# One core, a hybrid pooling and attention block: the value projection goes tile by tile, and ScalarE alone forms the modulated rows from the third tile on

## The chip, the core and the metric

The kernel runs on one core of a Trainium2 chip. That core has TensorE (PE in the profile, with its weight loads as PEld), VectorE (DVE), ScalarE (ACT), GpSimd (POOL) and the queue that issues most of its transfers, SyncE (SP). Every engine takes its own instructions strictly in the order in which they are written, and engines wait for one another with semaphores. The metric is the device time of one execution in microseconds (us).

## The reference, cut to what matters

One layer of a diffusion trunk, with 1024 latent tokens (8 tiles of 128 rows) and 256 context tokens (2 tiles), width 1024:

```python
hx = _rmsnorm(x, norm1[l]) * (1.0 + cx1) + sx1
hc = _rmsnorm(ctx, norm1[l]) * (1.0 + cc1) + sc1
yx, yc = _mixer(hx, hc, w_in[l], w_gk2[l], b_gk[l], w_pool[l], pool_scale[l], gla_gain[l], w_out[l], keep_ctx)
x = x + gx1 * yx
hx = _rmsnorm(x, norm2[l]) * (1.0 + cx2) + sx2
x = x + gx2 * _moe(hx.reshape(-1, D), w_router, router_bias, w1[l], w3[l], w2[l]).reshape(x.shape)
```

`_mixer` multiplies hx and hc by w_in and splits the product into u (pooling branch), q, k, v, the gate g and a rank-32 part r. From r come the decays (a small product, a log sigmoid, a cumulative sum over each chunk). A chunked linear attention with a state runs over q, k, v; its gated output and the pooled u go through w_out. `_moe` is a mixture of 16 experts, two for each token. The six modulation vectors (cx1, sx1, gx1 and so on) are silu(c) times w_mod plus a bias. All of it is float32.

## The kernel before, in words

**Precision by splitting.** A large product is made of three passes of a rounded format: a matrix is split into a high part (ScalarE copies it into the rounded format) and a low part (VectorE subtracts the high part from the original), and high*high, high*low and low*high are summed in one PSUM bank. So every group of the projection is 8 chunks of the inner dimension times 3, 24 matmuls, lines 1428 (v and g: one token tile against 256 columns) and 1431 (u, k, q: 128 columns against 512 or 256 tokens).

**Before the projection** (0 to 40 us) the first four 512-column pieces of w_mod (the shift and scale of the first norm) arrive by transfer and are multiplied with silu(c).

**The rows.** For each token tile t: `square(t)` on ScalarE sums the squares, GpSimd forms the reciprocal root, `scale_rows(t)` on VectorE scales the tile, and `turn_rows(t)` on TensorE (8 transposes, line 1355) writes it to PSUM banks 2 and 3. `hx_out(t)` then applies the modulation chunk by chunk: VectorE reads bank 2 (four instructions, line 905), ScalarE bank 3 (four instructions, line 646). `hx_high(t)` on ScalarE and `hx_low(t)` on VectorE split the result. The two banks are used once per tile, so turn_rows(t+1) waits until hx_out(t) is done.

**The projection loop.** All engines run over the same list of steps n, one projection group each (54 in all, the last 8 within the state phase). The list before is v (10 tiles for the first 256 columns, n = 0 to 9, then 10 tiles for the others, n = 10 to 19), u (n = 20 to 27), k (28 to 33), q (34 to 37), g (38 to 45, and 46 to 53). In the list each engine does, at step n, its share of several pipelines that are shifted against each other:

- TensorE: `late_turn`, then `proj(n)`, then turn_rows(n+2), `rank_rows` (r for several tiles, line 1401), `logits(n-10)` (line 1446) and `cumulate(n-13)` (line 1456).
- ScalarE: hx_out(n+2), `evacuate(n-1)` (line 700), hx_high(n+2), square(n+4), `decay_exp` (lines 680 to 684), `decays` (lines 669 to 673), `part_high` (line 659: the high half of the next columns of w_in).
- VectorE: hx_out(n+2), evacuate(n-1), scale_rows(n+3), hx_low(n+2), `softplus` (line 978), `late_row`, `late_sum`, steps of the pooling filter (`pool_steps`, lines 988 to 1022), and last `part_low` (line 915).

v groups are evacuated from PSUM by ScalarE (even tiles) and VectorE (odd tiles), u and g by ScalarE, k and q by VectorE. Banks 0 and 1 alternate for v, and from n = 20 on four banks are used, which is why the first u groups wait for `softplus` to have left banks 2 and 3.

**The late modulation.** The other eight 512-column pieces of w_mod arrive in 32 quarters of 512 KB (`load_late`, two buffers). `late_sum(q)` on VectorE multiplies and adds each quarter (two instructions, lines 951 and 953), `late_turn(i)` on TensorE (line 1465) sums over the partitions after each fourth quarter, and `late_row(i)` (line 966) adds the bias. The list `QUARTERS` says at which step n VectorE takes each quarter. TensorE's late_turn(i) waits for the last quarter of its piece (the semaphore increment at line 958) and for late_row(i-1).

**w_in in parts.** The columns of w_in come in eight parts of 1 MB (m = 0, 1: v; 2, 3: u; 4: k; 5: q; 6, 7: g), each split in two pieces (m, i). There is one high buffer and two low ones. `piece_free` says when the high buffer's piece may be overwritten, `pieces_at` at which step this is done.

**After the loop** comes the state phase (line 1486 transposes k, line 1498 multiplies it with v, VectorE carries the state; one g group runs in each of its steps), then attention outputs and the output projection, the routing, and from about 500 us on the experts (line 1644).

Of the kernel before, what the change touches and what calls it, by code (L numbers as in the profile page):

```python
# [23 lines left out]
F32 = mybir.dt.float32  # L24
# [6 lines left out]
P = 128  # L31
# [43 lines left out]
def hybrid_block(nc, x, c, ctx_in, c_ctx, w_mod, b_mod, norm1, norm2, w_in, w_gk2, b_gk, w_pool,  # L75
                 pool_scale, gla_gain, w_out, w_router, router_bias, w1, w3, w2, norm_f, inv_counts, out):
    with ExitStack() as stack:
# [47 lines left out]
        ROWS = NT - 1  # L125
        rows_at = [O_Q + t * D for t in range(ROWS)] + [O_V + NX * HALF]
        assert O_Q + ROWS * D == O_V
# [4 lines left out]
        with nc.sbuf_tensor("lead_u", [P, O_U], F32), nc.sbuf_tensor("rank_w", [P, KC, RANK2], F32) as w_r:  # L132
            pass
        sq0 = at(O_U + 256, None, D)
# [133 lines left out]
        NV = 2 * NT  # L268
        PB = 4

        def bank_of(n):

            return n % 2 if n < NV else n % PB

        def bank_before(n):

            if n < NV + 2:
                return n - 2
            return {NV + 2: -1, NV + 3: -1}.get(n, n - PB)

# [26 lines left out]

        def piece_free(m, i):

            if by_rows(m) and by_rows(m - 1):  # L310
                return (S["half_used"], m // 4 + 1) if i == 0 else (S["proj_done"], part_end[m - 1])
            if by_rows(m) or by_rows(m - 1):
                return S["proj_done"], part_end[m - 1]
            return S["proj_done"], block_end(m - 1, i)

        pieces_at = {}
        for m in range(1, len(parts)):
            for i in range(2):
                last = part_end[m - 1] if by_rows(m) or by_rows(m - 1) else block_end(m - 1, i)
                pieces_at.setdefault(last - 1, []).append((m, i))  # L320
# [13 lines left out]
        group_no = {g: n for n, g in enumerate(groups)}  # L334
# [60 lines left out]
        def _(sp):  # L395
# [7 lines left out]
            def load_part(m):  # L403
                if m >= 2:
                    sp.wait_ge(S["proj_done"], part_end[m - 2])
                col = parts[m][1]
                sp.dma_start(raw_part[m % 2].rearrange("p (k n) -> p k n", k=KC), win_v[:, :, col:col + HC]).then_inc(part_loaded[m % 2], 16)
# [15 lines left out]
            for t in range(2, NT):  # L423
                load_rows(t)
            load_part(1)
            for q in range(len(QUARTERS)):
                for m in range(2, 6):
                    if q == {2: 2, 3: 12, 4: 19, 5: 27}[m]:
                        load_part(m)
                load_late(q)  # L430
            load_part(6)
# [183 lines left out]
        def _(act):  # L615
# [24 lines left out]
            def hx_out(t):  # L640
                if t == 0:
                    act.wait_ge(S["mod_ready"], 2)
                which = 0 if t < NX else 1
                act.wait_ge(S["turned"], t + 1)
                for k in range(4, KC):
                    ins = act.activation(hx_full[t][:, k, :], ps[:, 3, (k - 4) * P:(k - 3) * P],
                                         ACT.Identity, bias=mod[:, 0, k, which:which + 1], scale=a1[:, k, which:which + 1])
                ins.then_inc(S["hx_a"], 1)

            def hx_high(t):  # L650
                act.wait_ge(S["hx_a"], t + 1)
                act.wait_ge(S["hx_v"], t + 1)
                act.activation(hx_h[:, t], hx_full[t], ACT.Copy).then_inc(S["hx_high"], 1)

            def part_high(m, i):
                act.wait_ge(part_loaded[m % 2], 16 * (m // 2 + 1))
                if m >= 1:
                    act.wait_ge(*piece_free(m, i))
                act.activation(piece(high_part[:, :], m, i), piece(raw_part[m % 2], m, i), ACT.Copy).then_inc(S["part_high"], 1)
# [27 lines left out]
            def evacuate(n):  # L687
                g = groups[n]
                if evac[n][0] != "ev_a":
                    return  # L690
                ev(n)
                if g[0] == "v":
                    out_ap, func = vals[:, g[2], g[1] * HC:(g[1] + 1) * HC], ACT.Copy
                elif g[0] == "u":
                    out_ap, func = uT[:, g[1], g[2] * HALF:(g[2] + 1) * HALF], ACT.Copy
# [15 lines left out]
            square(2)  # L711
            hx_out(1)
            hx_high(1)
            square(3)
            for n in range(group_no[("g", 1, 0)]):
                if n + 2 < NT:
                    hx_out(n + 2)
                if n >= 1:
                    evacuate(n - 1)
                if n + 2 < NT:  # L720
                    hx_high(n + 2)
                if n + 4 < NT:
                    square(n + 4)
# [164 lines left out]
        def _(dve):  # L888
# [24 lines left out]
            def part_low(m, i):  # L913
                dve.wait_ge(S["part_high"], 2 * m + i + 1)
                dve.tensor_tensor(piece(low_part[m % 2][:, :], m, i), piece(raw_part[m % 2], m, i),  # L915
                                  piece(high_part[:, :], m, i).bitcast(F32), ALU.subtract).then_inc(S["part_split"], 1)
# [18 lines left out]
            scale_rows(2)  # L935
            hx_out(1)
            hx_low(1)
            sc = ("s_chain", [0])
# [29 lines left out]
            def rank_out(n):  # L968

                first, count = rows_of(n)  # L970
                dve.wait_ge(S["r_done"], 1 + list(R_STEPS).index(n))
                for c in range(count):
                    dve.tensor_copy(rT[0:32, (first + c) * P:(first + c + 1) * P], ps[RANK2 * c:RANK2 * (c + 1), 6, 0:P])\
                        .then_inc(S["rT_ready"], 1)
# [71 lines left out]
            pool_from = group_no[("k", 1, 2)] + 2  # L1046
            for n in range(group_no[("g", 1, 0)]):
                if n + 2 < NT:
                    hx_out(n + 2)
# [4 lines left out]
                if n + 3 < NT:  # L1054
                    scale_rows(n + 3)
                if n + 2 < NT:
                    hx_low(n + 2)
                if 0 <= n - LAG_C < NT:
                    softplus(n - LAG_C)
                if n - 1 in late_turn_at:  # L1060
                    late_row(late_turn_at[n - 1])
# [6 lines left out]
                for m, i in pieces_at.get(n, ()):  # L1068
                    part_low(m, i)
# [274 lines left out]
        def _(pe):  # L1344
# [4 lines left out]
            def turn_rows(t):  # L1349
                pe.wait_ge(S["scaled"], t + 1)  # L1350
                if t >= 1:
                    pe.wait_ge(S["hx_a"], t)
                    pe.wait_ge(S["hx_v"], t)
# [37 lines left out]
            def rank_rows(n):  # L1391

                if n == 3:
# [4 lines left out]
                for k in range(KC):  # L1398
                    for part in range(2):
                        for c in range(count):  # L1400
                            ins = pe.matmul(ps[RANK2 * c:RANK2 * (c + 1), 6, 0:P], w_r[:, k, :],
# [4 lines left out]
            def proj(n):  # L1406
# [5 lines left out]
                elif n >= NV:  # L1412
                    pe.wait_ge(S["sp_ready"], n - NV + 7)
                w = [p_[:, :].rearrange("p (k n) -> p k n", k=KC) for p_ in (high_part, low_part[m % 2])]
# [8 lines left out]
                for k in range(KC):  # L1423
# [9 lines left out]
                    if k == 3 and n + 1 == part_end[m] and m in (0, 6):  # L1433
# [3 lines left out]
            def logits(t):  # L1437
                if t == 0:
# [3 lines left out]
                    pe.wait_ge(S["hx_v"], NT)  # L1442
# [25 lines left out]
            for n in range(group_no[("g", 1, 0)]):  # L1468
                if n in late_turn_at:
                    late_turn(late_turn_at[n])  # L1470
                proj(n)
                if n + 2 < NT:
                    turn_rows(n + 2)
# [247 lines left out]
```

## Time and profile before

| quantity | value |
|---|---|
| time, median of 3 runs | 1045.63 us (1043.37 to 1046.85) |
| the profiled execution | 1045.96 us, of which its span 1044.2 us |
| TensorE busy | 917.3 us (88%) |
| VectorE busy | 616.0 us (59%) |
| ScalarE busy | 388.5 us (37%) |
| GpSimd busy | 189.4 us (18%) |
| mean granted TensorE clock | 0.929 of full speed |

Busy time is an average over stages with different limits, so the profile is read here by stage: the stretch from the first projection group (40.35 us) to the first transpose of k (320.27 us), the state phase behind it, and the rest. A timeline row gives the start, the duration, engine, line, operation, output<-input, shapes and count; in brackets stands how long the engine was idle just before and which instruction ended the wait. Matmuls overlap, so what one costs is read from the distance between starts, not from its own duration.

### The profile page before, as it was taken

The numbers are of one execution on the slowest core, as the hardware profiler recorded it, in microseconds if no ns is written. First come the engines' busy times: TensorE is split into PE (matmuls) and PEld (weight loads), VectorE is DVE, ScalarE is ACT, GpSimd is POOL, SyncE is SP. The second block draws the span as 40 slices with busy tenths as digits, with TensorE's granted clock in tenths as the row PEclk, the third lists the DMA queues.
The fourth block names the chain that finished last, engine by engine and source line by source line (L and its number), as shares of the span: only waits on it lengthen the run. The fifth ranks groups of instructions, "written<-read, shape, count | busy, mean of one in ns | idle before, by whom it ended". The sixth has DMA issues, their size and how long they took to land. (4 is left out here: it accounts for less than half of the span.)

```text
span 1044.2 us, 15159 instructions
## 1 busy us (share of the span) xinstructions
PE 917.3 (88%) x5471; PEld 736.8 (71%) x5472; DVE 616.0 (59%) x814; ACT 388.5 (37%) x525; POOL 189.4 (18%) x210
## 2 busy tenths in 40 slices
PE   3788998899878999999973899999999999999960
PEld 1578776677677845656543788889888888988860
DVE  0554533557995634454436654949975467499933
ACT  1654453210012231212114153737754345477613
POOL 4110000000000001000100122323342232234322
PEclk8888998999989989999995699999999999999985
DMA  9800424552111362111156658898998886699928
GB/s 335 325 2 1 123 88 128 176 180 73 51 41 33 133 239 81 57 65 41 41 193 230 252 147 244 264 323 249 371 380 260 243 266 204 186 339 381 333 38 344
DMA packets 81136, 194.73 MB, mean 186 GB/s; under 512 B 3893, under 2 KB 12218, under 8 KB 81098
## 3 DMA queue, kind: packets, MB, share of 16 engines
q1 hardware_dynamic: 68736, 152.05, 41.4%
q0 software_dynamic: 7616, 25.34, 9.9%
q10 hardware_dynamic: 4746, 16.82, 4.2%
q8 instruction: 25, 0.41, 0.2%
q14 instruction: 13, 0.11, 0.0%
HBM read 168.50 MB, written 25.71 MB: 186 GB/s over the span
## 5 line engine op out<-in xcount | busy, mean ns | idle before, releaser
L1568 PE MATMUL ps<-arena 128*128 128x512 f32 x256 | 113.3, 595 | 0.0
L1644 PE MATMUL ps<-w3h,xTh 128*128 128x256 f32 x368 | 105.9, 288 | 0.0
L1428 PE MATMUL ps<-high,hx_h 128*128 128x256 f32 x288 | 89.0, 309 | 18.7 <-DVE low_even L915 6.7
L1644 PE MATMUL ps<-w3h,xTl 128*128 128x256 f32 x368 | 104.2, 283 | 0.0
L1644 PE MATMUL ps<-w3l,xTh 128*128 128x256 f32 x368 | 104.1, 283 | 0.0
L1428 PE MATMUL ps<-high,hx_l 128*128 128x256 f32 x288 | 85.8, 298 | 0.0
L1568 PEld LDWEIGHTS ps<-arena 128*128 128x128 f32 x256 | 47.4, 190 | 54.4 <-issue 53.6
L1279 DVE TENSOR_TENSOR w1l<-raw,w1h 128x2048 fp32r<-128x2048 f32 x30 | 68.6, 2287 | 29.0 <-ACT w1h L811 29.0
L811 ACT ACTIVATE w1h<-raw 128x2048 fp32r (+1 forms) x32 | 61.1, 1913 | 58.4 <-PE ps L1644 39.4
L1644 PE MATMUL ps<-w2h,hTh 128*128 128x512 f32 x184 | 76.9, 418 | 1.3 <-DVE hTl L1292 0.9
L1428 PEld LDWEIGHTS ps<-high,hx_h 128*128 128x128 f32 x288 | 60.0, 208 | 25.5 <-issue 11.7
L1644 PE MATMUL ps<-w1h,xTh 128*128 128x512 f32 x184 | 72.7, 395 | 3.4 <-DVE xTl L1272 3.4
L1644 PE MATMUL ps<-w1l,xTh 128*128 128x512 f32 x184 | 72.5, 394 | 0.0
L1644 PE MATMUL ps<-w1h,xTl 128*128 128x512 f32 x184 | 72.3, 393 | 0.0
L1644 PE MATMUL ps<-w2l,hTh 128*128 128x512 f32 x184 | 72.2, 392 | 0.0
L1644 PE MATMUL ps<-w2h,hTl 128*128 128x512 f32 x184 | 72.1, 392 | 0.0
L811 ACT ACTIVATE w2h<-raw 128x2048 fp32r (+1 forms) x32 | 61.1, 1918 | 28.9 <-PE ps L1644 21.1
L1279 DVE TENSOR_TENSOR w2l<-raw,w2h 128x2048 fp32r<-128x2048 f32 x32 | 71.7, 2283 | 0.0
L1644 PEld LDWEIGHTS ps<-w3l,xTh 128*128 128x128 f32 x368 | 70.5, 192 | 0.9
L1644 PEld LDWEIGHTS ps<-w3h,xTh 128*128 128x128 f32 x368 | 70.4, 191 | 0.9
L1279 DVE TENSOR_TENSOR w3l<-raw,w3h 128x2048 fp32r<-128x2048 f32 x31 | 70.9, 2286 | 0.0
L1644 PEld LDWEIGHTS ps<-w3h,xTl 128*128 128x128 f32 x368 | 70.5, 192 | 0.0
(259 smaller groups left out, 1961.9 us busy)
## 6 DMA issues: line engine op xcount, KB each, us to landing
raw<-in_w_dram SPq DMA_DIRECT2D x48, 2048.0 KB, 13.5
arena<-in_w_mod_dram SPq DMA_DIRECT2D x32, 512.0 KB, 3.7
arena<-in_w_mod_dram SPq DMA_DIRECT2D x4, 2048.0 KB, 16.0
arena<-in_w_in_dram SPq DMA_DIRECT2D x8, 1024.0 KB, 5.4
x_rows<-arena ACTq DMA_DIRECT2D x9, 512.0 KB, 2.6
hx_rows<-arena ACTq DMA_DIRECT2D x9, 512.0 KB, 2.6
arena<-in_x_dram SPq DMA_DIRECT2D x8, 512.0 KB, 12.6
arena<-in_w_out_dram SPq DMA_DIRECT2D x2, 2048.0 KB, 8.3
```

Of the source, the lines that this page charges most:

```text
L811: act.activation(half_of(j, w_hi[j][:, :], k), half_of(j, raw[:, bass.ds(base, UNIT)], k), ACT.Copy).then_inc(w_high[j], 1)
L1279: dve.tensor_tensor(half_of(j, w_lo[j][:, :], k), half_of(j, raw[:, bass.ds(base, UNIT)], k), half_of(j, w_hi[j][:, :], k).bitcast(F32), A ...
L1428: ins = pe.matmul(out_ap, hx[x_][:, t, k, :], w[w_][:, k, :], start=(k == 0 and i == 0), stop=(k == KC - 1 and i == 2))
L1568: ins = pe.matmul(ps[:, 5 + h, :], m, w[:, k, :], start=(k == 0), stop=(k == KC - 1))
L1644: ins = pe.matmul(out_ap, parts[l][:, lhs], w_parts[w][:, cols], start=start and n == 0, stop=stop and n == 2)
```

## The change

The order of the v groups becomes tile by tile: n = 0 is tile 0 against the first 256 columns, n = 1 tile 0 against the others, and so on to n = 19. With it:

- A tile is transposed every second step (`turn_after`), after proj(n); ScalarE's hx_out comes one step later (`hx_at`). For tiles 0 and 1 both engines still form four chunks each; from tile 2 on ScalarE forms all eight and VectorE none.
- ScalarE evacuates every v group.
- Part 1 of w_in is loaded ahead of the rows of tiles 3 to 9, gets a high buffer of its own (`high_v1`) and is split before the loop. Part 2 gets a raw buffer of its own, part 5 a high buffer of its own (`high_q`), so pieces 2, 5, 6 are split earlier than at the end of the part before.
- Rows of tiles 8 and 9 reuse the places of tiles 0 and 1 and are loaded after these are transposed.
- Banks 0 and 1 alternate up to n = 27; the first use of banks 2 and 3 is n = 30 and 31.
- logits and cumulate run 15 and 17 steps behind instead of 10 and 13; the rank groups follow n = 7, 15, 18 instead of 3, 7, 9 and use bank 4.
- VectorE takes one late quarter a step from n = 4 to 19 and two a step from n = 20 to 27 (before: one a step from 10 to 19, two from 20 to 27, one from 28 to 33). TensorE's late_turn stands behind proj(n), not ahead of it. On VectorE part_low comes ahead of late_sum and the pooling steps, late_row last.

```diff
-LAG_L, LAG_C = 10, 13
-R_STEPS = {3: (0, 4), 7: (4, 4), 9: (8, 2)}
+LAG_L, LAG_C = 15, 17
+R_STEPS = {7: (0, 4), 15: (4, 4), 18: (8, 2)}
...
-QUARTERS = ([10 + q for q in range(10)] + [20 + q // 2 for q in range(16)] + [28 + q for q in range(6)])
+QUARTERS = ([4 + q for q in range(16)] + [20 + q // 2 for q in range(16)])
...
-        groups = ([("v", h, t) for h in range(2) for t in range(NT)] + [("u", p, g) for p in range(NG) for g in range(2)]
+        groups = ([("v", h, t) for t in range(NT) for h in range(2)] + [("u", p, g) for p in range(NG) for g in range(2)]
...
+            if m == 7:
+                return (S["half_used"], 1) if i == 0 else (S["proj_done"], part_end[6])
+            if m in (2, 6):
+                return S["proj_done"], part_end[m - 2]
+            if m == 5:
+                return S["proj_done"], group_no[("k", 1, 0)]
             return S["proj_done"], block_end(m - 1, i)
...
+                step = {2: part_end[0] - 1, 5: group_no[("k", 1, 0)] + i, 6: group_no[("q", 0, 1)], 7: part_end[6] - 1}.get(m)
...
+        turn_after = {1: 2, **{2 * (t - 2): t for t in range(3, NT)}}
+        hx_at = {n + 1: t for n, t in turn_after.items()}
+        scale_at = {2 * (t - 2) - 1: t for t in range(3, NT)}
+        square_at = {2 * (t - 2) - 3: t for t in range(4, NT)}
...
-            on_act = g[0] in "ug" or (g[0] == "v" and g[2] % 2 == 0)
+            on_act = g[0] in "ugv"
...
-                for k in range(4, KC):
-                    ins = act.activation(hx_full[t][:, k, :], ps[:, 3, (k - 4) * P:(k - 3) * P],
+                for k in range(4 if t < 2 else 0, KC):
+                    ins = act.activation(hx_full[t][:, k, :], ps[:, 2 + k // 4, (k % 4) * P:(k % 4 + 1) * P],
...
-                for m, i in pieces_at.get(n, ()):
-                    part_low(m, i)
+                if n - 1 in late_turn_at:
+                    late_row(late_turn_at[n - 1])
...
             for n in range(group_no[("g", 1, 0)]):
+                proj(n)
+                if n in turn_after:
+                    turn_rows(turn_after[n])
                 if n in late_turn_at:
                     late_turn(late_turn_at[n])
-                proj(n)
-                if n + 2 < NT:
-                    turn_rows(n + 2)
                 if n in R_STEPS:
                     rank_rows(n)
```

ScalarE's queue early in the v groups. `hx_f<-ps,mod,a` is hx_out, `arena<-ps 128x256` an evacuation, `hx_h<-hx_f` hx_high, `arena,stat<-arena` a square. Before:

```order
L646 ACTIVATE hx_f<-ps,mod,a 128x128 x4
L700 ACTIVATE arena<-ps 128x256
L653 ACTIVATE hx_h<-hx_f 128x1024
L632 ACTIVATE arena,stat<-arena 128x1024
L646 ACTIVATE hx_f<-ps,mod,a 128x128 x4
```

After:

```order
L673 ACTIVATE hx_f<-ps,mod,a 128x128 x8
L729 ACTIVATE arena<-ps 128x256
L680 ACTIVATE hx_h<-hx_f 128x1024
L659 ACTIVATE arena,stat<-arena 128x1024
L729 ACTIVATE arena<-ps 128x256
```

Per tile there are now eight chunks and two evacuations in ScalarE's queue, where there were four chunks and one evacuation for every second tile.

VectorE's queue around the split of part 6, the first columns of g (`low_even<-arena,high 128x1024 x2`), in the q groups (`arena<-ps,arena` evacuates a q group; the others are pooling). Before:

```order
L1041 SCALAR_TENSOR_TENSOR arena<-ps,arena 128x4x128 x2
L1011 TENSOR_TENSOR arena<-arena 128x16x68
L1011 TENSOR_TENSOR arena<-arena 128x16x64
L1015 TENSOR_TENSOR arena<-arena,icnt 128x16x64
L1019 TENSOR_TENSOR arena<-arena 128x1024
L915 TENSOR_TENSOR low_even<-arena,high 128x1024 x2
L1041 SCALAR_TENSOR_TENSOR arena<-ps,arena 128x4x128 x2
```

After:

```order
L1074 SCALAR_TENSOR_TENSOR arena<-ps,arena 128x4x128 x2
L946 TENSOR_TENSOR low_even<-arena,high 128x1024 x2
L1028 TENSOR_TENSOR arena<-arena 128x1024
L1035 MEMSET arena 128x16x4
L1036 MEMSET arena 128x16x4
L1037 TENSOR_TENSOR arena<-arena,icnt 128x16x64
```

The split moved from behind the pooling of step 37 to the front of step 35, right behind the evacuation of the first q group.

SyncE's queue at the start (`in_w_in` is a part of w_in, `in_x` and `in_ctx` the rows, `in_w_mod` of 128x2x512 a late quarter). Before:

```order
L407 DMA arena<-in_w_in_dram 128x8x256
L398 DMA arena<-in_x_dram 128x1024 x6
L398 DMA arena<-in_ctx_dram 128x1024 x2
L407 DMA arena<-in_w_in_dram 128x8x256
L415 DMA arena<-in_w_mod_dram 128x2x512 x2
```

After:

```order
L430 DMA arena<-in_w_in_dram 128x8x256
L418 DMA arena<-in_x_dram 128x1024
L430 DMA arena<-in_w_in_dram 128x8x256
L418 DMA arena<-in_x_dram 128x1024 x5
L418 DMA arena<-in_ctx_dram 128x1024 x2
L438 DMA arena<-in_w_mod_dram 128x2x512 x11
```

Part 1 moved ahead of seven row tiles, and eleven late quarters now come before part 2.

## Rows read from the trace of the kernel before

**Rows 1.** The page, the chain that ended last, shares of the span by engine.

```profile
PE 37%; DMA 5%; DVE 3%; issue 1%; ACT 1%; SPq 0%; DVEq 0%; POOLq 0%; POOL 0%; ACTq 0%
```

**Rows 2.** Stages: length, busy us (instructions) of each engine, granted clock, DMA share, GB/s.

```profile
40.35:320.27 279.92, 243.04 (x1605) 203.93 (x1605) 161.43 (x237) 87.01 (x206) 15.63 (x33) 0.92 0.29 91
366.00:1044.20 678.20, 613.83 (x3362) 486.33 (x3362) 416.62 (x453) 278.88 (x279) 159.64 (x136) 0.94 0.66 222
227.90:295.70 67.80, 55.11 (x245) 43.72 (x243) 55.66 (x74) 6.95 (x7) 3.33 (x6) 0.92 0.28 90
```

**Rows 3.** Waits of TensorE, 40 to 321 us: us in total, times, longest.

```profile
PE ps L1465 <- DVEq L958: 10.1, 4, 3.3
PE ps L1446 <- DVE arena L978: 8.5, 4, 4.9
PE ps L1428 <- DVE low_even L915: 6.7, 1, 6.7
PE ps L1428 <- DVE arena L1029: 6.6, 3, 3.1
PE ps L1428 <- ACT arena L700: 3.9, 2, 1.9
PE ps L1428 <- DVE hx_l L911: 1.5, 2, 1.1
```

**Rows 4.** Timeline of TensorE, starts at which projection groups and small groups follow each other.

```profile
44.47 1.04 PE L1355 MATMUL ps<-ident,arena 128*128 128x128 f32 x8
...
59.88 0.47 PE L1428 MATMUL ps<-high,hx_h 128*128 128x256 f32 x1 [1.79 <-DVE arena L1029]
...
64.35 1.04 PE L1355 MATMUL ps<-ident,arena 128*128 128x128 f32 x8
65.32 0.43 PE L1401 MATMUL ps<-hx_h,rank_w 128*32 128x128 f32 x8
...
68.95 0.38 PE L1428 MATMUL ps<-high,hx_h 128*128 128x256 f32 x1
...
71.92 1.04 PE L1355 MATMUL ps<-ident,arena 128*128 128x128 f32 x8
...
126.66 1.02 PE L1465 MATMUL ps<-wp,ones 128*1 128x512 f32 x2
...
130.67 1.12 PE L1446 MATMUL ps<-arena 33*128 33x512 f32 x2
131.72 1.16 PE L1456 MATMUL ps<-tri,arena 128*128 128x129 f32 x8
...
250.13 0.39 PE L1431 MATMUL ps<-hx_h,high 128*128 128x512 f32 x1
...
255.57 0.39 PE L1431 MATMUL ps<-hx_h,high 128*128 128x512 f32 x1
```

**Rows 5.** Timeline of ScalarE, one tile's share: chunks, evacuation, high part, square.

```profile
65.49 1.50 ACT L646 ACTIVATE hx_f<-ps,mod,a 128x128 f32<-128x128 f32 x4 [3.67 <-PE ps L1355]
66.87 0.40 ACT L700 ACTIVATE arena<-ps 128x256 f32<-128x256 f32 x1
67.13 1.08 ACT L653 ACTIVATE hx_h<-hx_f 128x1024 fp32r<-128x1024 f32 x1
68.08 1.08 ACT L632 ACTIVATE arena<-arena 128x1024 f32<-128x1024 f32 x1
```

**Rows 6.** Timeline of VectorE: chunks and low part of tile 1.

```profile
42.81 1.36 DVE L905 TENSOR_SCALAR hx_f<-ps,a,mod 128x128 f32<-128x128 f32 x4
45.36 1.22 DVE L911 TENSOR_TENSOR hx_l<-hx_f,hx_h 128x1024 fp32r<-128x1024 f32 x1 [1.19 <-ACT hx_h L653]
```

**Rows 7.** VectorE's late sums, 40.35 to 320.27 us: count, busy us, mean ns, idle before.

```profile
L953 DVE SCALAR_TENSOR_TENSOR wp<-arena,silu_c,wp 128x512 f32<-128x512 f32 x56 | 41.9, 748 | 8.6 <-DMA arena<-in_w_mod_dram 6.7 <-DVE wp L953 0.2
```

**Rows 8.** The page, DMA issues: count, KB each, median us to landing.

```profile
arena<-in_w_mod_dram SPq DMA_DIRECT2D x32, 512.0 KB, 3.7
arena<-in_x_dram SPq DMA_DIRECT2D x8, 512.0 KB, 12.6
```

**Rows 9.** Timeline of TensorE, second step of the state phase.

```profile
329.43 1.77 PE L1498 MATMUL ps<-arena,ktok 128*64 128x128 f32 x16 [2.49 <-DVE state L1100]
```

More of the change, by code:

```diff
@@ L123, in hybrid_block @@
         uT = at(O_U, "p (g t) -> p g t", NG * NX * P, g=NG)
-        ROWS = NT - 1
-        rows_at = [O_Q + t * D for t in range(ROWS)] + [O_V + NX * HALF]
-        assert O_Q + ROWS * D == O_V
+        rows_at = [O_K + 3 * D, O_K + 4 * D, O_Q, O_Q + D, O_K, O_K + D, O_K + 2 * D, O_V + NX * HALF]
+        rows_at += rows_at[0:2]
+        assert O_K + 5 * D == O_V
         rows = [at(off, None, D) for off in rows_at]
@@ L268, in hybrid_block @@
         NV = 2 * NT
+        group_no = {g: n for n, g in enumerate(groups)}
         PB = 4
+        RING = NV + 2 * NG
         def bank_of(n):
-            return n % 2 if n < NV else n % PB
+            return n % 2 if n < RING else n % PB
         def bank_before(n):
-            if n < NV + 2:
-                return n - 2
-            return {NV + 2: -1, NV + 3: -1}.get(n, n - PB)
+            return n - 2 if n < RING + 2 else {RING + 2: -1, RING + 3: -1}.get(n, n - PB)
         def rows_of(n):
@@ L306, in piece, with high_for, raw_for @@
             return v[:, 4 * i:4 * (i + 1), :] if by_rows(m) else v[:, :, i * P:(i + 1) * P]
+        def high_for(m):
+            return high_of.get(m, high_part)
+        def raw_for(m):
+            return raw_u0 if m == 2 else raw_part[m % 2]
         def piece_free(m, i):
[L310 to L313, printed above, removed]
+            if m == 7:
[4 more added lines that the diff above has]
+                return S["proj_done"], group_no[("k", 1, 0)]
             return S["proj_done"], block_end(m - 1, i)
         pieces_at = {}
-        for m in range(1, len(parts)):
+        for m in range(2, len(parts)):
             for i in range(2):
-                last = part_end[m - 1] if by_rows(m) or by_rows(m - 1) else block_end(m - 1, i)
-                pieces_at.setdefault(last - 1, []).append((m, i))
+                step = {2: part_end[0] - 1, 5: group_no[("k", 1, 0)] + i, 6: group_no[("q", 0, 1)], 7: part_end[6] - 1}.get(m)
+                pieces_at.setdefault(block_end(m - 1, i) - 1 if step is None else step, []).append((m, i))
+        turn_after = {1: 2, **{2 * (t - 2): t for t in range(3, NT)}}
+        hx_at = {n + 1: t for n, t in turn_after.items()}
+        scale_at = {2 * (t - 2) - 1: t for t in range(3, NT)}
+        square_at = {2 * (t - 2) - 3: t for t in range(4, NT)}
         late_turn_at = {QUARTERS[4 * i + 3] + 1: i for i in range(8)}
@@ L422, in _ @@
             load_part(0)
-            for t in range(2, NT):
+            load_rows(2)
+            load_part(1)
+            for t in range(3, NT):
+                if t >= 8:
+                    sp.wait_ge(S["turned"], t - 7)
                 load_rows(t)
-            load_part(1)
             for q in range(len(QUARTERS)):
-                for m in range(2, 6):
-                    if q == {2: 2, 3: 12, 4: 19, 5: 27}[m]:
+                for m in range(2, 5):
+                    if q == {2: 11, 3: 18, 4: 26}[m]:
                         load_part(m)
                 load_late(q)
+            load_part(5)
             load_part(6)
@@ L934, in _ @@
             part_low(0, 1)
-            scale_rows(2)
             hx_out(1)
             hx_low(1)
+            part_low(1, 0)
+            part_low(1, 1)
+            scale_rows(2)
             sc = ("s_chain", [0])
@@ L1053, in _ @@
                     evacuate(n - 1)
[L1054 to L1057, printed above, removed]
+                if n in scale_at:
+                    scale_rows(scale_at[n])
+                if n in hx_at:
+                    hx_low(hx_at[n])
                 if 0 <= n - LAG_C < NT:
                     softplus(n - LAG_C)
-                if n - 1 in late_turn_at:
-                    late_row(late_turn_at[n - 1])
+                for m, i in pieces_at.get(n, ()):
+                    part_low(m, i)
                 for q, at_step in enumerate(QUARTERS):
@@ L1432, in proj @@
                                             start=(k == 0 and i == 0), stop=(k == KC - 1 and i == 2))
-                    if k == 3 and n + 1 == part_end[m] and m in (0, 6):
+                    if k == 3 and n + 1 == part_end[m] and m == 6:
                         ins.then_inc(S["half_used"], 1)
```

60 lines of the change are left out of this document (35 added, 25 removed).

## The prediction, made before the run

> **What bounds the kernel now.** I read the chain that ended last first: of the shares of the span that it gives to engines, TensorE has 37% and no other engine over 3% [rows 1]. So TensorE's time counts, and what it waits for. Then the busy time by stage. The change touches the stretch from 40.35 to 320.27 us, 279.92 us long, in which TensorE is busy 243.04 us at a mean granted clock of 0.92; VectorE is busy 161.43 us and ScalarE 87.01 us of it [rows 2], so both have room on average. What lies behind 366 us (678.2 us) keeps its instructions and their order; I cost it at nothing, since its transfers are issued on events of that later work itself.
>
> The third view is the list of TensorE's waits in that stretch [rows 3]: 10.1 us at the late turns, 8.5 at the logits, 6.7 in front of the first g group, and 6.6 + 3.9 + 1.5 = 12.0 between v groups. Together 37.3 us.
>
> The fourth is the distance between starts. A v group takes 71.92 - 68.95 = 2.97 us at full clock, and the group that starts at 59.88, right behind a wait, takes 64.35 - 59.88 = 4.47 us [rows 4]. So there are two speeds, and a group that runs slow costs about 1.5 us more. Full clock is the 2.4 GHz level, the other 1.2 GHz.
>
> **TensorE's work in the stretch**, at full clock [rows 4]: 28 v and g groups and 2 short k groups by 2.97 = 89.1; 16 groups of u, k, q by 255.57 - 250.13 = 5.44, 87.0; 8 tiles of transposes by 65.32 - 64.35 = 0.97, 7.8; 3 rank groups by 68.95 - 65.32 = 3.63, 10.9; 10 logits by 1.05, 10.5; 10 cumulations by 1.1, 11.0; 8 late turns by 1.0, 8.0. The last two are the rows' own lengths, a little high. Sum 224.3. With 37.3 of waits that leaves 279.9 - 224.3 - 37.3 = 18.3 us, which is what the slow clock costs. The change removes no work here; it can only take from 37.3 + 18.3 = 55.6 us.
>
> **The change, part by part.**
>
> **v groups.** Before, a tile is turned after proj(n), ScalarE and VectorE form its chunks (1.5 and 1.36 us for four), and only then do they evacuate group n, whose bank or whose successor proj(n+1) waits for. That is the 12.0 us. After, a tile is turned every second group. ScalarE then needs 8 chunks: 66.87 - 65.49 = 1.38 us for four, so 2.76, and 0.40 for the evacuation [rows 5]: 3.2 us after the turn the bank is free. TensorE meanwhile runs one other group, 2.97 us. The wait is about 0.3 us for a tile where nothing else lies between, and none where a rank group (3.63) or a late turn (1.0) does: some four tiles, and 0.5 for the first of them where chunks of tiles 2 and 3 queue up. I take 1.5 us in all. ScalarE's load per tile: 2.76 + 2 x 0.3 + 0.95 + 1.15 = 5.5 us, against 2 x 2.97 + 0.97 = 6.9 us of TensorE. It stays under, with 1.4 us to spare. VectorE has per tile a scaling, a low part (1.22) and two late quarters (4 x 0.75), some 5 us.
>
> **The start of the loop.** Part 1 must be split before group 1. Group 0 ends at 44.47 [rows 4]. Tile 1's chunks on VectorE end near 42.7 (42.81 + 1.36 before, where a scaling of 0.7 came first [rows 6]); ScalarE then does the high part of tile 1 and a square (about 1 us each, rows 5) and two halves of part 1, of the same shape. The first half is high at about 46.0, low 1.22 later: 47.3. TensorE waits 47.3 - 44.5 = 2.9 us. Of the transfers: part 1 now stands behind about 12 of the 17 MB that are moved by 48 us, so it lands near 35 and is not what comes last. Ends: 1 us if the square comes early and cheap, 6 if the data are late.
>
> **Late quarters.** They start at step 4, and late_turn stands behind proj. For turns 0 to 6 VectorE then has two groups of TensorE for four quarters: from step 20 on at least 11 us for 4 x 1.5 = 6 us of sums [rows 7] and 1.2 of part_low. The landing of 3.7 us [rows 8] with two buffers fits in. Not so for the last: at step 27 part_low waits for group 27 to end (its piece is free only then), 1.04 + 1.22 us, then come two quarters (3.1) and late_row (0.7), 6.1 us, and TensorE reaches the turn after the short group 28, 2.97 us. Wait 3.2 us, in the manner of the longest before, 3.3 [rows 3]. Turn 6 has under a microsecond to spare. So 10.1 becomes 3.2 (ends 1 and 7).
>
> **Logits.** Before, softplus stood behind an evacuation on VectorE that waits for the group just done: 1.2 us three times, and 4.9 in front of the u groups, behind the split of part 2. After, VectorE evacuates no v group, so softplus stands behind nothing that waits for the group just done, and part 2 is split behind group 18 while TensorE runs a rank group and group 19. 8.5 becomes 0 (other end 4: decays and the exponentials in one ScalarE step take 3.2 us).
>
> **First g group.** The split moves from behind the pooling to step 35. 6.7 becomes 0. What is late next is VectorE itself. In the stretch 227.9 to 295.7 it is busy 55.7 us [rows 2]. Its late sums and rows in it, seven quarters by 1.5, leave (about 10.7); three more pooling steps enter (about 6): 51 us from step 30 to the evacuation of group 37. Group 41 needs that bank, and TensorE gets there in 8 x 5.44 + 3 x 2.97 = 52.4 us. It is a dead heat; I take a wait of 1 us (ends 0 and 5).
>
> **State phase.** Before, pooling ran into it, and TensorE waited 2.49 us for VectorE, with the clock low behind it [rows 9]. After, only one pooling step of 2.5 us is left behind the last split, and it fits. Gain 2.5 + 0.5 = 3.0 us.
>
> **The clock.** 18.3 us are lost to it now, behind some of the sixteen waits of rows 3. After, there are three waits over 1 us. Group 0 is slow either way (1.2); one slow group behind the wait at the start, one behind the last late turn, one near group 41, and one or two in the v groups with their small gaps make 1.2 + 4.2 x 1.5 = 7.5 us (ends 2 and 18).
>
> **A rule against it.** Rows first: four chunks take VectorE 1.36 us and ScalarE 1.50 [rows 5, 6], so the move of four chunks costs ScalarE 1.4 and frees VectorE of as much. The Trainium skill, page "ScalarE: Activation LUTs", section "Rules for kernel authors", says to do multiply and add on VectorE, which it puts at up to about three times faster per element in bf16. If that held for these chunks, each would take ScalarE 1 us, its load per tile would be about 10.7 us, and the v groups would take 30 us more: an estimate of 1033 us from that page's factor. Here the data are float32 and the rows show 10%, so the sum goes by the rows.
>
> **The sum.** Waits after: 1.5 + 2.9 + 3.2 + 0 + 1 = 8.6 us; clock 7.5. The stretch: 224.3 + 8.6 + 7.5 = 240.4, from 279.9: a gain of 39.5. With the state phase 42.5. From the profiled execution, 1045.96: 1003.5; its own time lies 0.3 above the median of the three runs, so 1003.
>
> **The rivals.**
>
> *The clock does not recover.* The v groups keep gaps, small but at each tile. All 18.3 us stay: 224.3 + 8.6 + 18.3 = 251.2, gain 28.7 + 3 = 31.7, time 1014. For it: a slow stretch before came at times after only 1.2 us of waiting. Against: most groups between the 1.2 us waits ran at 2.97. The Trainium skill, page "TensorE: Matmul & The Clock Gate", section "A second HAM failure mode: psum-queue depth-cycling", tells of such short idles between groups that keep the clock going up and down; by it the 18.3 would stay, and this case is its.
>
> *All waits vanish.* ScalarE frees the bank in time, VectorE wins the dead heat, the start costs 1 us and the clock 2: 224.3 + 4 + 2 = 230.3, gain 49.6 + 3, time 993.
>
> *A new bound eats part of it.* VectorE, with sums ahead of the low parts of tiles, or ScalarE with 5.5 us of 6.9, falls behind by 1.5 us per tile and 5 us in k and q: 8 x 1.5 + 5 = 17 us more, time 1020. For it: VectorE is in order, and a late quarter that isn't there stops the low part of the next tile. Against: 3.7 us of landing against some 7 us for two quarters.
>
> *Slower than before.* The same mechanism, from a landing that makes it decide: sixteen quarters are now taken in the v groups, two per landing. If the pair costs landing + 3.1 us, the eight pairs must take 42 us more than 8 x 7 us, 12.3 us each, so the landing must be over 9 us. The rows of tiles landed in 12.6 us in the crowded first 48 us [rows 8]; at that price the pair takes 15.7 us and the time is 1003 + 8 x 8.7 - 2 = 1072. Against: the transfers that crowd are over by then, and the same quarters took 3.7.
>
> *It does not do what it says* (the old waits stay because something I read as free is not): 1046.
>
> **Chances.** Forecast (998 to 1009) 0.50; clock (1010 to 1016) 0.18; all vanish (990 to 997) 0.12; new bound (1017 to 1035) 0.14; no difference 0.03; slower 0.03. Time 1003; the range from 992 to 1019 leaves out about 0.18. About 0.3% is what can be told from no change. Faster by more 0.94, within 0.03, slower 0.03. The 1033 of the page on ScalarE, with 0.01, lies within the new bound's case and could be left out of it.
>
> **What would show it.** Right: in the list of waits of TensorE the late turn has one long wait of about 3 us, logits none, the first g group none; the first k transpose starts 36 to 44 us earlier; the longest wait early is 2.5 to 3.5 us in front of group 1, on the split of part 1; eight chunks on ScalarE take about 2.8 us. Wrong: a wait of a microsecond or more at each tile, a clock in the stretch of 0.92 or less, waits on VectorE's low parts of tiles, or a longer stretch behind 366 us.

## The result, and the profile after

The changed kernel took 1000.41 us (median of 4 runs, 997.16 to 1001.54) beside 1044.62 us of the kernel before: ratio 0.957, 95% interval 0.954 to 0.960, 4.3% faster. The forecast was 1003 in 992 to 1019, and faster. The profiled execution took 1000.64 us, its span is 998.9.

The chain that ended last has the same shape as [rows 1], with TensorE's share larger, since what shrank is the time in which it waited:

```profile
PE 41%; DMA 3%; DVE 3%; issue 1%; ACT 0%; SPq 0%; DVEq 0%; POOLq 0%; POOL 0%; ACTq 0%
```

The stages of the kernel after, to be read as [rows 2]: length, busy us (instructions) of TensorE, its loads, VectorE, ScalarE and GpSimd, granted clock, DMA share, GB/s. The first is the stretch of the projections, the second the state phase up to the first scores, the third the rest:

```profile
41.94:281.54 239.60, 228.74 (x1604) 193.54 (x1605) 150.24 (x197) 100.40 (x248) 17.01 (x33) 0.97 0.34 104
281.54:325.03 43.49, 39.16 (x394) 35.90 (x393) 30.40 (x113) 10.28 (x20) 0.00 (x0) 1.00 0.33 119
325.03:998.90 673.87, 611.28 (x3362) 485.35 (x3362) 415.05 (x447) 278.79 (x279) 160.16 (x136) 0.94 0.66 222
```

And the last two stages of the kernel before, cut at the same instructions:

```profile
320.27:367.60 47.33, 40.80 (x394) 37.34 (x393) 32.99 (x115) 10.27 (x20) 0.00 (x0) 0.96 0.30 108
367.60:1044.20 676.60, 613.83 (x3362) 486.30 (x3362) 415.15 (x447) 278.88 (x279) 159.64 (x136) 0.94 0.66 221
```

The span is 45.3 us shorter: the stretch 279.92 - 239.60 = 40.3, the state phase 47.33 - 43.49 = 3.8, the rest 676.60 - 673.87 = 2.7, less 1.6 by which the first group started later (41.94 instead of 40.35). The last two are scatter: a second profile of the changed kernel has the start at 40.17, then stages of 236.78, 43.49 and 677.26 us. Over all profiles of this study the first group starts between 39.8 and 42.5 us and the rest lasts 673.9 to 677.8 us.

TensorE's waits in the kernel after (us in total, times, longest), the answer to [rows 3]:

```profile
PE ps L1496 <- DVE state L999: 4.6, 2, 4.2
PE ps L1459 <- DVE low_odd L946: 2.5, 1, 2.5
PE ps L1459 <- DVE arena L1074: 2.4, 1, 2.4
PE ps L1459 <- ACT arena L729: 1.2, 3, 0.4
PE ps L1459 <- DVE hx_l L942: 0.4, 1, 0.4
PE ps L1386 <- issue: 0.2, 1, 0.2
```

Line 1496 is the late turn (1465 before), 1459 a group of v or g, 729 ScalarE's evacuation, 946 the low half of a part, 942 hx_low, 1074 VectorE's evacuation of q, 999 late_row. The 0.4 us for hx_low end where the stretch begins, at 41.94, and are left out; the sum is 10.9 us. The 37.3 us of the kernel before count the same 0.4 us at 40.35, so within the stretch it is 10.9 from 36.9. No wait in front of the logits is left, and none for the split of the first g columns. The granted clock of the stretch went from 0.92 to 0.97.

Where the longest stand, in TensorE's timeline:

```profile
48.89 0.58 PE L1459 MATMUL ps<-high_v,hx_h 128*128 128x256 f32 x1 [2.46 <-DVE low_odd L946]
...
68.91 0.39 PE L1459 MATMUL ps<-high,hx_h 128*128 128x256 f32 x1 [0.39 <-ACT arena L729]
...
205.38 1.81 PE L1496 MATMUL ps<-wp,ones 128*1 128x512 f32 x2 [4.24 <-DVE state L999]
...
265.56 0.39 PE L1459 MATMUL ps<-high,hx_h 128*128 128x256 f32 x1 [2.36 <-DVE arena L1074]
```

And one tile on ScalarE, the answer to [rows 5]: eight chunks, the evacuation that group 6 waits for, the high part, the square:

```profile
65.69 2.90 ACT L673 ACTIVATE hx_f<-ps,mod,a 128x128 f32<-128x128 f32 x8 [1.71 <-PE ps L1386]
68.44 0.42 ACT L729 ACTIVATE arena<-ps 128x256 f32<-128x256 f32 x1
68.70 1.10 ACT L680 ACTIVATE hx_h<-hx_f 128x1024 fp32r<-128x1024 f32 x1
69.65 1.10 ACT L659 ACTIVATE arena<-arena 128x1024 f32<-128x1024 f32 x1
```

The chunks take 68.44 - 65.69 = 2.75 us (forecast 2.76), the evacuation ends at 68.86, and TensorE goes on at 68.91. ScalarE stood idle for 1.71 us before this tile's chunks.

### The profile page after: what moved, and what is told of

Same layout as the page of the kernel before. It is cut to its first block and busy times, and to the rows that moved or that the text cites. A ratio compares the mean times of both kernels' runs of the same rounds, so it can differ in the third digit from the quotient of the medians.

```text
span 998.9 us, 15160 instructions
## 1 busy us (share of the span) xinstructions
PE 902.6 (90%) x5471; PEld 726.0 (73%) x5472; DVE 602.1 (60%) x772; ACT 401.7 (40%) x567; POOL 191.3 (19%) x210
## 5 line engine op out<-in xcount | busy, mean ns | idle before, releaser
L842 ACT ACTIVATE w3h<-raw 128x2048 fp32r (+1 forms) x32 | 61.3, 1917 | 22.4 <-PE ps L1675 20.1
L1459 PE MATMUL ps<-high,hx_h 128*128 128x256 f32 x208 | 61.7, 297 | 3.9 <-DVE arena L1074 2.4
L591 POOL COPY block_tok<-slot_tok 128x1 int32 (+1 forms) x24 | 27.2, 1135 | 178.1 <-PE ps L1669 146.1
```

Of the source, the lines that this page charges most:

```text
L591: pool.tensor_copy(block_tok[:, :], slot_tok[:, bass.ds(b, 1)]).then_inc(S["tok_ready"], 1)
L842: act.activation(half_of(j, w_hi[j][:, :], k), half_of(j, raw[:, bass.ds(base, UNIT)], k), ACT.Copy).then_inc(w_high[j], 1)
L1459: ins = pe.matmul(out_ap, hx[x_][:, t, k, :], w[w_][:, k, :], start=(k == 0 and i == 0), stop=(k == KC - 1 and i == 2))
```

## The experiments

Every kernel ran five rounds beside the kernel before on the same chip, unless said otherwise. The changed kernel once more:

> The changed kernel once more, as the yardstick for the others. All theories: 998 to 1002 us, the stretch of the projections about 240 us long at a granted clock near 0.97.

1000.7 us (997.68 to 1003.33), ratio 0.9576 (0.9552 to 0.9601); stretch 236.78. This is what the others are measured against.

**Who forms the chunks.**

```diff
-                for k in range(4 if t < 2 else 0, KC):
+                for k in range(4, KC):
...
+                if n in hx_at:
+                    hx_out(hx_at[n])
```

(the second on VectorE; the waits count all tiles' chunks again.)

> The new order stays, but VectorE forms four of the eight chunks of every tile again, as in the kernel before. Theory A (the new order with one turn for two groups carries the gain, and who forms the chunks hardly matters, since both engines have room): the 1.2 us of waits for ScalarE's evacuation in the v groups go, nothing else moves, 997 to 1001 us. Theory B (VectorE's strict order makes the difference: its chunks stand behind late sums that wait, so the next turn and the high parts come late): new waits of about a microsecond per tile, 1004 to 1015 us.

1000.13 us, ratio 0.9572 (0.9552 to 0.9591): no difference from the changed kernel, and theory A in its time, though not in "nothing else moves". The 1.2 us for evacuations went, and a wait of 1.3 us came at a late turn (line 1498 here), because VectorE now stands with its chunks ahead of the late sums. Its waits:

```profile
PE ps L1498 <- DVE state L999: 4.3, 2, 3.9
PE ps L1461 <- DVE arena L1074: 2.4, 1, 2.4
PE ps L1461 <- DVE low_odd L946: 2.3, 1, 2.3
PE ps L1498 <- DVEq L991: 1.3, 1, 1.3
```

So forming the chunks on ScalarE alone is worth nothing that can be measured. What is left of the change is the new order of the groups with the schedules that go with it; the order by itself was not run.

**How much room ScalarE has.** From tile 2 on four chunks are formed twice, the first time into a place that is overwritten.

```diff
+                for k in range(4 if t >= 2 else 0):
+                    act.activation(hx_h[:, t, k, :], ps[:, 2, k * P:(k + 1) * P],
+                                   ACT.Identity, bias=mod[:, 0, k, which:which + 1], scale=a1[:, k, which:which + 1])
```

> From tile 2 on ScalarE forms four chunks twice (the first copy is overwritten), 1.38 us more per tile, 6.9 us of work per tile beside 6.9 us of TensorE. Theory A (the evacuation behind the chunks sets TensorE's wait in the v groups, now 0.4 us, and ScalarE's room is 1.4 us per tile): the waits grow by 1.0 to 1.4 us per tile where nothing covers them and by 0.6 where a late turn does, 5 to 7 us in all, plus up to 6 us of clock: 1005 to 1012 us. Theory B (ScalarE has ample room, since it is busy 42% of the stretch): under 1 us, 1000 to 1001.

1011.3 us, ratio 0.9672 (0.9651 to 0.9693), 10.6 us slower. The waits for the evacuation grew from 1.2 to 6.7 us, and 1.6 came in front of a turn:

```profile
PE ps L1462 <- ACT arena L732: 6.7, 5, 1.8
PE ps L1499 <- DVE state L1002: 4.6, 2, 4.2
PE ps L1389 <- issue: 1.6, 1, 1.6
```

The longest wait, 1.8 us, is the 0.4 of the changed kernel and the 1.38 that the second copy takes. So the forecast's chain from turn over chunks and evacuation to the next group is real; in the changed kernel it binds already, by 0.4 us at three tiles. Theory A holds in its size too.

**The last late turn.**

```diff
-        late_turn_at = {QUARTERS[4 * i + 3] + 1: i for i in range(8)}
+        late_turn_at = {QUARTERS[4 * i + 3] + 1 + (i == 7): i for i in range(8)}
```

> The last late turn stands behind the second short k group instead of the first. Theory A (the 4.2 us wait there is on TensorE's path, VectorE being done 4 us after the first short group): TensorE runs the 2.9 us group inside the wait, about 1.5 us of waiting are left, and less of the clock is lost behind it: 3 to 5 us faster, 996. Theory B (VectorE is the bound from there to the g groups, so the wait only moves to the evacuation in front of the fourth g group, 2.4 us now): no change, 1000, with a wait there of 5 us.

996.2 us, ratio 0.9533 (0.9515 to 0.9551). The wait fell from 4.24 to 1.37 us and the one in front of the fourth g group stayed:

```profile
PE ps L1459 <- DVE arena L1074: 2.3, 1, 2.3
PE ps L1496 <- DVE state L999: 1.8, 2, 1.4
```

Theory A: the wait was TensorE's own, not a shadow of the next. VectorE begins its pooling earlier as well, 8.4 us behind the start of group 28 and not 13.7, because the evacuation of group 29, behind which it starts, comes earlier.

**The order before the loop.** On ScalarE (VectorE likewise):

```diff
             hx_out(1)
-            hx_high(1)
-            square(2)
             part_high(1, 0)
+            hx_high(1)
             part_high(1, 1)
+            square(2)
             square(3)
```

> Before the loop ScalarE splits the first half of part 1 ahead of tile 1's high part and the second ahead of the square, VectorE likewise. Theory A (the 2.5 us in front of group 1 are engine queues, as the prediction had it, and part 1 has long landed): the wait falls from 2.5 to under 0.5 us and the clock gives back up to 1.3: 2 to 4 us faster, 997 to 998. Theory B (the landing of part 1 is what comes last): the wait stays over 2 us, 1000.

997.0 us, ratio 0.9549 (0.9528 to 0.9569), and the wait in front of group 1 is gone from the list altogether. The data had landed; the queues of the two engines were what came last.

**The pooling spread.**

```diff
-                    for _ in range(3 if n < group_no[("g", 0, 0)] else 1):
+                    for _ in range(3 if n < 36 else 2 if n < 41 else 1):
```

> Two pooling steps in each of the steps 36 to 40 instead of three in 36 and 37 and one behind. Theory A (VectorE's queue up to the evacuation of group 37 is what the fourth g group waits for): about 4 us less in front of it, the 2.4 us wait goes and one slow group (1.3 us) with it: 997. Theory B (the pooling taken out there is missing later and TensorE waits in the state phase, as in the kernel before): 1000 or more, with a wait for VectorE behind 281 us.

995.4 us, ratio 0.9529 (0.9509 to 0.9549). The wait in front of the fourth g group is gone, and the state phase is as long as before, 43.49 us. Theory A.

**The late quarters back to steps 10 to 33** (three rounds, four executions; the loads of the parts go back with them).

```diff
-QUARTERS = ([4 + q for q in range(16)] + [20 + q // 2 for q in range(16)])
+QUARTERS = ([10 + q for q in range(10)] + [20 + q // 2 for q in range(16)] + [28 + q for q in range(6)])
```

> The late quarters (and the loads of the parts between them) go back to the steps of the kernel before, 10 to 33; all else is the changed kernel. Theory A (the sum was right that VectorE has no spare time from step 28 on): six quarters and two rows, about 10 us of VectorE, come back into the k groups, and the wait in front of the fourth g group or at late turns grows by 6 to 10 us: 1006 to 1012 us. Theory B (VectorE is busy 81% there and absorbs it): under 2 us, 1000 to 1002.

1013.21 us, ratio 0.9713 (0.9679 to 0.9747), 12.5 us slower, a little more than theory A said. The waits at late turns are 7.1 us, those for VectorE's evacuations 5.2:

```profile
PE ps L1495 <- DVEq L990: 7.1, 3, 2.9
PE ps L1458 <- DVE arena L1073: 5.2, 2, 3.2
PE ps L1458 <- ACT arena L728: 2.0, 5, 0.4
```

All waits of the stretch come to 17.7 us, 6.6 more than in the other profile of the changed kernel. The stretch is 14.2 us longer (250.99 instead of 236.78), at a granted clock of 0.96 instead of 0.99, so more than half of the loss is clock. The place is only in part the one that theory A named: at the two last of these late turns and the two evacuations TensorE waits 10.7 us, 3.7 more than in the changed kernel at its late turns and its evacuation. Most of the other waits are new ones around 105 us, 1.6 at a late turn and 1.0 in front of a turn of rows, and 0.8 more for ScalarE's evacuations.

**The split of the first g columns back behind the pooling** (three rounds, four executions).

```diff
-6: group_no[("q", 0, 1)], 7: part_end[6] - 1}
+6: part_end[5] - 1, 7: part_end[6] - 1}
```

(and on VectorE part_low of part 6 behind the pooling steps.)

> The split of part 6, the first columns of g, goes back to step 37, on VectorE behind the pooling. Theory A: TensorE waits for it in front of the first g group, 8 to 10 us since VectorE is later relative to TensorE than before, while the 2.4 us in front of the fourth go: 1006 to 1010 us. Theory B (only the old 6.7 us come back, less the 2.4): 1004 to 1005.

1007.1 us, ratio 0.9632 (0.9604 to 0.9661). Theory A: the wait is longer than the 6.7 us of [rows 3], and the one in front of the fourth g group is gone:

```profile
PE ps L1463 <- DVE low_even L946: 8.7, 1, 8.7
```

**What took the waits in front of the logits away.** First VectorE evacuates the odd tiles' v groups again (three rounds, four executions):

```diff
-            on_act = g[0] in "ugv"
+            on_act = g[0] in "ug" or (g[0] == "v" and g[2] % 2 == 0)
```

> In the changed kernel VectorE evacuates the v groups of odd tiles again. Theory A (the prediction's: softplus no longer stands behind an evacuation that waits for the group just done): the waits of 1.2 us in front of logits come back at steps 16 to 20, 2 to 4 us in all, 1002 to 1005. Theory B (it is the longer lag: VectorE does the softplus that a logit waits for one step earlier, so the evacuation ahead of it is of a group that is long done): no such wait, 999 to 1001.

1000.08 us beside 1043.24, ratio 0.9588 (0.9562 to 0.9614): no wait in front of a logit, no loss. Theory B: it was not the move of the evacuations that took the waits away here. In VectorE's timeline of this kernel the evacuation of group 19 (line 1062), for which VectorE had to wait 0.24 us, stands right ahead of a softplus (line 1011), as in the kernel before, and nobody waits for it:

```profile
132.69 0.42 DVE L1062 COPY arena<-ps 128x256 f32<-128x256 f32 x1 [0.24 <-PE ps L1459]
133.09 0.69 DVE L1011 SCALAR_TENSOR_TENSOR arena<-ps,arena 128x512 f32<-128x512 f32 x1
```

Then the same with one number changed besides (two rounds, nine executions), which makes the softplus, the cumulation and the exponentials follow the logits by three steps, as before the change, and not by two:

```diff
-LAG_L, LAG_C = 15, 17
+LAG_L, LAG_C = 15, 18
```

> As the run in which VectorE evacuates the odd tiles' v groups, and besides cumulate, softplus and the exponentials run 18 steps behind instead of 17, so three behind the logits as in the kernel before, not two. Theory A (the distance of the two lags, not who evacuates, took the waits in front of the logits away: at three, the softplus that logits(t) waits for stands in VectorE's next step, behind splits and sums that wait for the group just done): waits in front of logits come back, four or more and 4 to 10 us in all, 1004 to 1012. Theory B (something else took them away): none, 999 to 1001.

1045.33 us beside 1043.84, ratio 1.0023 (1.0003 to 1.0043). One step of lag gives back the whole gain, far more than the 4 to 12 us that theory A put on it. The stretch is 281.51 us long, and TensorE waits 32 us in front of eight logits:

```profile
PE ps L1477 <- DVE arena L1011: 32.0, 8, 7.3
40.09:321.60 281.51, 240.34 (x1605) 202.26 (x1606) 153.98 (x207) 98.07 (x238) 17.01 (x33) 0.92 0.29 91
```

How one of the two longest comes about, ScalarE, VectorE and then TensorE in their timelines:

```profile
160.81 1.06 ACT L686 ACTIVATE high<-arena 128x1024 fp32r<-128x1024 f32 x1 [2.96 <-PE ps L1462]
```

```profile
161.90 1.23 DVE L946 TENSOR_TENSOR low_odd<-arena,high 128x1024 fp32r<-128x1024 f32 x1 [10.63 <-ACT high L686]
163.04 3.21 DVE L986 SCALAR_TENSOR_TENSOR wp<-arena,silu_c,wp 128x512 f32<-128x512 f32 x4
166.60 0.68 DVE L999 TENSOR_TENSOR state<-ps,ktok 1x512 f32<-1x512 f32 x1 [0.35 <-DVE wp L986]
167.21 0.67 DVE L1011 SCALAR_TENSOR_TENSOR arena<-ps,arena 128x512 f32<-128x512 f32 x1
```

```profile
168.03 2.04 PE L1477 MATMUL ps<-arena 33*128 33x512 f32 x2 [7.32 <-DVE arena L1011]
```

TensorE ends a u group at step n. Only then may ScalarE write the next high half (1.1 us), VectorE the low half (1.2), then in its order two quarters (3.2) and a late row (0.7): all that is VectorE's step n. The softplus stands in its step n + 1. With a distance of three, logits(t), which TensorE runs at step n, needs that softplus; with two it needs the one in step n, ahead of the split. So where TensorE's step n depends on another engine's step n + 1, everything that the other engine's step n waits for is put into TensorE's path.

The split is not the only such thing. Three of the eight waits, 4.1 us each, stand behind late sums that wait for the late turn of the same step, and one, 1.2 us, stands behind an evacuation of the group just done, here VectorE and then TensorE for each:

```profile
147.46 0.48 DVE L984 TENSOR_SCALAR wp<-arena,silu_c 128x512 f32<-128x512 f32 x1 [8.86 <-PE ps L1496]
151.41 1.09 PE L1477 MATMUL ps<-arena 33*128 33x512 f32 x2 [4.07 <-DVE arena L1011]
...
137.58 0.42 DVE L1062 COPY arena<-ps 128x256 f32<-128x256 f32 x1 [5.36 <-PE ps L1459]
138.75 1.09 PE L1477 MATMUL ps<-arena 33*128 33x512 f32 x2 [1.21 <-DVE arena L1011]
```

The second pair is a wait of the kernel before come back, 1.21 us as there (lines 1029 and 1446 were what is 1062 and 1477 here):

```profile
123.38 0.42 DVE L1029 COPY arena<-ps 128x256 f32<-128x256 f32 x1 [4.08 <-PE ps L1428]
124.55 1.09 PE L1446 MATMUL ps<-arena 33*128 33x512 f32 x2 [1.21 <-DVE arena L978]
```

So with three steps between logits and softplus VectorE's evacuations do cost time, with two they don't. They account for some 1.6 of the 32 us; the same lag with ScalarE evacuating was not run. And 26.8 of the 32 us fall among the u groups, where the new lag of 15 has put five logits; in the kernel before the last logits ran ahead of the u groups. The splits and late turns in those steps make the waits so much longer than the old 8.5 us.

**All three repairs together.**

> The last late turn one group later, the pooling spread and the new order before the loop, together on the changed kernel. Theory A (the three waits are separate places on TensorE's path): the gains of 4.2, 5.3 and 3.7 us add, 987 to 989 us. Theory B (the first two are one shortage of VectorE, taken away twice, and the slow clock comes back elsewhere): 991 to 995.

988.91 us (987.87 to 991.69) beside 1043.24, ratio 0.9476 (0.9455 to 0.9498). Singly the ratios fell from 0.9576 by 0.0043, 0.0027 and 0.0047, together by 0.0100, against a sum of 0.0117: they add, within what the intervals allow. The stretch is 227.47 us long at a granted clock of 0.99:

```profile
42.48:269.95 227.47, 224.30 (x1604) 190.23 (x1605) 151.67 (x198) 100.40 (x248) 16.59 (x33) 0.99 0.35 109
```

**And with the chunks shared.**

> The same with VectorE forming four of eight chunks of every tile again. Theory A (who forms the chunks hardly matters; 1.2 us of waits for evacuation go, 1.3 come at a late turn): within 2 us of the run with all three. Theory B (with the other waits gone, VectorE's load counts): 3 us or more slower.

987.87 us (987.42 to 989.7), ratio 0.9471 (0.9448 to 0.9493). The same again: who forms the chunks does not matter. Both of these beat the changed kernel by about 1%.

## Why the prediction was right, and where not

- **The bound.** TensorE's work in the stretch was put at 224.3 us. From the profile after, 239.6 less 10.9 of waits and less the slow groups (two at the start 1.3 each, 1.7 at and behind the last late turn, 1.6 from 265.56 us on: 5.9) is 222.8. Too high by 1.5, as the text had said of two of its rows. With 222.8 the clock's cost before was 279.9 - 36.9 - 222.8 = 20.2, and not 18.3.
- **v groups.** 12.0 us were to become 1.5. Measured 1.2 for evacuations and 0.2 in front of a turn. The longer chain on ScalarE showed the mechanism.
- **Start.** 2.9 forecast, 2.5 in one profile and 2.7 in the other, on the engine queues, as said; the reordering took all of it.
- **Late turns.** 10.1 to 3.2; measured 4.6. The mechanism was right and the term mis-sized: from the end of group 27 to the end of late_row(6) it took 7.1 us, not 6.1, because VectorE stood idle for 0.74 us ahead of late_row and began the low half 1.35 us behind group 27 and not 1.04; and turn 6, which was to have under a microsecond to spare, waited 0.4.

The rows of that place, VectorE in the kernel after:

```profile
199.46 1.23 DVE L946 TENSOR_TENSOR low_even<-arena,high 128x1024 fp32r<-128x1024 f32 x1 [3.62 <-ACT high L686]
200.60 3.22 DVE L986 SCALAR_TENSOR_TENSOR wp<-arena,silu_c,wp 128x512 f32<-128x512 f32 x4
204.56 0.68 DVE L999 TENSOR_TENSOR state<-ps,ktok 1x512 f32<-1x512 f32 x1 [0.74 <-DVE wp L986]
```

- **Logits.** 8.5 to 0, measured 0, by luck. The step that failed reads "VectorE evacuates no v group, so softplus stands behind nothing that waits for the group just done". The evacuations were indeed behind the three old waits of 1.2 us, but with them back in the changed kernel nothing changed. What keeps the waits away is the distance between two lags, two steps and not three, which the text did not weigh; with three, and VectorE's evacuations, they are 32 us in the new order. The range for this term, 0 to 4, named ScalarE as its risk and not this.
- **First g group.** 6.7 to 0 and a dead heat behind it of 0 to 5 us, put at 1; measured 2.4. TensorE took 52.3 us from step 30 on, as forecast (52.4). VectorE's 51 us were right as busy time, 51.4, but they were taken for its whole time: it also stood idle for 3.2 us in short gaps, and the evacuation of group 37 ended after 54.6 us. That the pooling ahead of it is what can be moved, the spread showed.
- **State phase.** 3.0 forecast, 3.8 measured: the 2.49 us wait of [rows 9] is gone, and the clock there is 1.00 instead of 0.96. What is left beside the wait is 1.3 us, not 0.5.
- **Clock.** 18.3 to 7.5; measured 5.9 in one profile and, with 222.8 of work and 11.1 of waits, 2.9 in the other. The clock rival (1014) did not come about: the gaps of 0.4 us at the tiles left the groups at full speed. On this the rule of the Trainium skill, "TensorE: Matmul & The Clock Gate", section "A second HAM failure mode: psum-queue depth-cycling", that short idles between groups keep the clock going up and down, is not borne out at gaps of that size. In the run with the longer chain slow groups come back: behind its three waits of 1.8 us in the v groups two groups ran slow (63.88 to 68.09 and 74.06 to 78.24) and one at full speed (103.37 to 106.35).
- **The Trainium skill's rule for ScalarE** ("ScalarE: Activation LUTs", section "Rules for kernel authors") is stated for bf16; carried over to these float32 chunks it would have given the 1033 of the prediction. The eight chunks took ScalarE 2.75 us, 0.34 each, and the run with VectorE's share back gave the same time.
- **The rest** was costed at nothing and is within scatter.
- **The total** is closer than its terms: forecast of the gain 42.5 us, measured 44 to 45. The waits came out 2.3 us too low (8.6 against 10.9), the work 1.5 and the clock at least 1.6 too high, and these make up for one another, which is luck.
- **A slip.** In the rival "slower than before" 1003 + 8 x 8.7 - 2 is 1071, not 1072. Nothing hangs on it.

## What to carry to other kernels

When several engines walk one list of steps, look at the distance between the lags and not only at the lags: a result that an engine uses at step n must be made in the other engine's step n or earlier, and ahead of whatever in that step waits for step n itself. Busy time did not show it: VectorE is busy 153.98 us of the stretch in both kernels with its evacuations back, lag 17 and lag 18, and they took 1000 and 1045 us. And after such a change cost the queues of the other engines instruction by instruction, idle gaps with them, up to whatever TensorE waits for next: the three long waits that were left, for a split, a late_row and an evacuation, stood at the end of such queues, and moving work by a step or two at each took 1.2% more off.

## What the runs showed of the hardware that was not expected

The same wait does not always cost the same. Behind 2.46 us of waiting, group 1 ran slow in one profile of the changed kernel (48.89 to 53.17, 4.28 us), and behind 2.72 us it ran at full speed in the other profile of the same kernel (47.13 to 50.11, 2.98 us). Its row there:

```profile
PE ps L1459 <- DVE low_odd L946: 2.7, 1, 2.7
```

Between these two profiles the stretch differs by 2.8 us (239.60 and 236.78), and nearly all of it is two such groups, group 1 and the one behind the wait for the evacuation of q, slow in the first and at full speed in the second. Four chunks of float32 out of PSUM took ScalarE 1.50 us and VectorE 1.36 [rows 5, 6], closer than I would have guessed.
